# Token-major layer norms in the second half of a two-model float32 forward pass on one Trainium2 core

## The reference

```python
def layer_norm(x, g, b):
    xf = x.astype(jnp.float32)
    mu = jnp.mean(xf, axis=-1, keepdims=True)
    var = jnp.mean(jnp.square(xf - mu), axis=-1, keepdims=True)
    y = (xf - mu) * lax.rsqrt(var + LN_EPS) * g.astype(jnp.float32) + b.astype(jnp.float32)
    return y.astype(x.dtype)
...
    h = layer_norm(x, ln_in_g, ln_in_b)
    for l in range(DEPTH_2):
        mix = token_mix(h, positions, w_in[l], b_in[l], pool_w[l], pool_scale[l], w_pool_out[l],
...
        h = layer_norm(DEEPNORM_ALPHA * h + mix, ln1_g[l], ln1_b[l])
        ffn = conv_ffn(h, w_up[l], ffn_dw_w[l], ffn_dw_b[l], w_down[l])
        h = layer_norm(DEEPNORM_ALPHA * h + ffn, ln2_g[l], ln2_b[l])
    return h
```

## Time and profile before

| what | value |
|---|---|
| median of 3 runs (lowest, highest) | 2410.09 us (2407.65, 2414.35) |
| profiled execution: its own time | 2415.38 us |
| its span in the trace | 2413.2 us |
| PE busy | 2281.4 us, 95% |
| DVE, ACT, POOL busy | 1550.5, 1141.5, 348.5 us |
| mean granted PE clock | 0.962 of full speed |

### The profile page before, as it was taken

How to read it: one execution, slowest core, us unless ns; L and a number is a source line. 1 busy time by engine, 2 the same in 40 slices (tenths; PEclk the granted TensorE clock), 3 DMA queues, 4 the chain that set the end, 5 groups by cost and what they waited for, 6 DMA issues and landing times.

```text
span 2413.2 us, 45770 instructions
## 1 busy us (share of the span) xinstructions
PE 2281.4 (95%) x18326; PEld 2203.9 (91%) x18326; DVE 1550.5 (64%) x2039; ACT 1141.5 (47%) x1478; POOL 348.5 (14%) x448
## 2 busy tenths in 40 slices
PE   8999998999999999999999998988899998989998
PEld 7899997899999999999989997886899987878997
DVE  6865547665467775554876545866777466866764
ACT  5653345544355555433664434434365353445542
POOL 0011100022000000220301100930012038000110
PEclk9999998999999999999999999998999998889999
DMA  6356542366544444665435653542466542515651
GB/s 208 125 145 190 192 131 94 88 191 187 185 157 146 145 153 123 186 187 186 151 123 157 191 191 93 153 134 76 122 175 188 187 132 88 191 53 140 188 182 65
DMA packets 431038, 362.12 MB, mean 150 GB/s; under 512 B 20524, under 2 KB 404144, under 8 KB 430904
## 3 DMA queue, kind: packets, MB, share of 16 engines
q1 hardware_dynamic: 429128, 358.79, 48.5%
q0 software_dynamic: 1264, 0.71, 0.1%
q10 hardware_dynamic: 512, 0.72, 0.1%
HBM read 359.12 MB, written 1.05 MB: 149 GB/s over the span
## 4 chain that ended last, share of the span: by engine, by line
PE 79%; DVE 9%; POOL 6%; ACT 3%; issue 1%; DMA 0%; SPq 0%; ACTq 0%; POOLq 0%; DVEq 0%
PE bank L495 70%; POOL hT L1405 4%; DVE weights_lo L1984 3%; POOL Z L1407 2%; PE bank L598 2%; PE bank L526 1%; PE bank L842 1%; PE bank L1037 1%; PE bank L1069 1%; ACT weights_hi L1443 1%; PE bank L755 1%; PE bank L856 1%; PE bank L1050 1%; PE bank L779 1%; PE bank L733 0%
## 5 line engine op out<-in xcount | busy, mean ns | idle before, releaser
L1984 DVE TENSOR_TENSOR weights_lo<-weights,weights_hi 128x2048 fp32r<-128x2048 f32 x343 | 788.7, 2299 | 483.3 <-ACT weights_hi L1443 481.1
L495 PE MATMUL bank<-h_hi,weights_hi 128*128 128x256 f32 x3648 | 1045.3, 287 | 46.7 <-DVE h_lo L2524 16.6
L495 PE MATMUL bank<-h_lo,weights_hi 128*128 128x256 f32 x3648 | 1034.2, 283 | 0.0
L495 PE MATMUL bank<-h_hi,weights_lo 128*128 128x256 f32 x3648 | 1033.6, 283 | 0.0
L1443 ACT CAST weights_hi<-weights 128x2048 fp32r<-128x2048 f32 x343 | 654.5, 1908 | 524.6 <-PE bank L495 516.3
L495 PEld LDWEIGHTS bank<-h_hi,weights_hi 128*128 128x128 f32 x3648 | 701.6, 192 | 57.9 <-issue 51.4
L495 PEld LDWEIGHTS bank<-h_lo,weights_hi 128*128 128x128 f32 x3648 | 701.6, 192 | 1.5 <-issue 1.4
L495 PEld LDWEIGHTS bank<-h_hi,weights_lo 128*128 128x128 f32 x3648 | 701.0, 192 | 0.0
L495 PE MATMUL bank<-hid_hi,weights_hi 128*128 (+1 forms) x1056 | 295.5, 280 | 0.0
L495 PE MATMUL bank<-hid_lo,weights_hi 128*128 (+1 forms) x1056 | 295.4, 280 | 0.0
L495 PE MATMUL bank<-hid_hi,weights_lo 128*128 (+1 forms) x1056 | 295.4, 280 | 0.0
(11 more groups left out here) (350 smaller groups left out, 2738.9 us busy)
## 6 DMA issues: line engine op xcount, KB each, us to landing
weights<-in_f_w_gu SPq DMA_DIRECT2D x176, 512.0 KB, 5.0
weights<-in_f_w_out SPq DMA_DIRECT2D x88, 512.0 KB, 4.2
weights<-in_w_up SPq DMA_DIRECT2D x88, 512.0 KB, 4.9
weights<-in_w_in SPq DMA_DIRECT2D x82, 512.0 KB, 4.6
weights<-in_c_w_qkv SPq DMA_DIRECT2D x72, 512.0 KB, 4.5
weights<-in_a_w_qkv SPq DMA_DIRECT2D x48, 512.0 KB, 4.6
weights<-in_w_down SPq DMA_DIRECT2D x44, 512.0 KB, 4.1
weights<-in_a_w_o SPq DMA_DIRECT2D x16, 512.0 KB, 4.1
```

Of the source, the lines that this page charges most:

```text
L495: mm = nc.tensor.matmul(out, x, y, start=(first and n == 0), stop=(last and n == 2), skip_group_check=True)
L1984: v_.tensor_tensor(w_lo[slot][:], raw[slot][:], w_hi[slot][:].bitcast(F32), ALU.subtract).then_inc(lo_ready, 1)
```

## The change

The residual stream of the second model is kept with tokens in the partitions (`x_t`, the same memory as `xT`, read as 2 tiles of 128 tokens x 1024 features).

- The projections in front of a norm (`f_w_out` of the last layer, `w_o_2`, `w_down_2`) run through the new `deep_tokens`: the activations are the stationary operand, the weights the moving one, 512 columns per matmul, 24 matmuls per unit. The four banks are (token tile, half of the features).
- In the last feed-forward of the first model `residual_to_banks` puts the residual into the banks ahead of the projection, by 16 float32 matmuls with the identity.
- DVE's add (`add_tokens`) sums over features in its accumulator; ACT squares with the negative mean as bias and sums in its accumulator; mean, root and reciprocal are 128 x 1. The final RMS norm is folded in: squares straight from the banks, then one DVE instruction that scales and sums.
- The normalized rows are turned back by 16 transposes; DVE applies gain and offset as it takes them out of the banks, ACT rounds, DVE makes `h_lo`.
- POOL multiplies the gain into `x_t` and adds the offset (two instructions of 128 x 2048), `residual`, for the next norm's residual.
- SP loads the gains and offsets, repeated over the partitions, 512 KB each: 3 such loads in the first model's last feed-forward, 2 at the head and 2 at the tail of each `ffn2`.
- The last norm ends in token order, so `end` goes; four stores of 256 KB take the place of two of 512 KB.

```diff
+            def residual_to_banks():
+
+                for tt in range(NT):
+                    for half in range(2):
+                        x = open_item(2 * tt + half)
+                        for kk in range(4):
+                            nc.tensor.matmul(banks[x.bank][:, kk * P:(kk + 1) * P], xT[:, 4 * half + kk, tt * P:(tt + 1) * P],
+                                             ident[:], start=(kk == 0), stop=False, skip_group_check=True)
+                        token_items.append(x)
...
+            def deep_tokens(name, l, n_units, src, tag, bank0, ready, begun=()):
...
+                def step(u, n, last):
+                    w = parts(u, 1024)
+                    for tt in range(NT):
+                        for half in range(2):
...
+                            for j in range(2):
+                                mm = product(banks[x.bank][:], [y[:, (2 * n + j) * T + tt * P:(2 * n + j) * T + (tt + 1) * P] for y in src],
+                                             [y[:, j, 512 * half:512 * half + 512] for y in w], fresh and j == 0, last and j == 1)
+                            if last:
+                                close(mm, x, *([u] if tt + half == 2 else []))
...
-                if source:
-                    m = sums(at, xT, lambda j: pe.wait_ge(bank_free[source[j].bank], source[j].free))
-                else:
-                    m = sums(at, xT, lambda j: pe.wait_ge(y_ready, 2 * j + 2))
-                v = sums(at + 1, sq, lambda j: pe.wait_ge(squares_ready, count(squares_ready)))
...
+                            for kk in range(2):
+                                k = 2 * j + kk
+                                mm = nc.tensor.transpose(banks[at + j][:, kk * T + tt * P:kk * T + (tt + 1) * P],
+                                                         x_t[:, tt, k * P:(k + 1) * P], ident[:])
+                            if tt:
+                                close(mm, xs[j])
...
+                    if u.index in gains_at:
+                        where, g, b, l = gains_at[u.index]
+                        if l is None:
+                            sp.dma_start(final_gain, vector_row("final_norm", None)).then_inc(gains_landed[where], 16)
+                        for z, name in enumerate((g, b)):
+                            sp.dma_start(gains[where][:, z, :], vector_row(name, l)).then_inc(gains_landed[where], 16)
...
+            def residual(tag, where, landed_now):
+
+                x = items[tag][3]
+                pool.wait_ge(pe_done, x.done)
+                pool.wait_ge(gains_landed[where], landed_now)
+                g, b = (gains[where][:, z, :].unsqueeze(1).to_broadcast([P, NT, D]) for z in range(2))
+                gp.tensor_tensor(x_t[:], x_t[:], g, ALU.mult).then_inc(residual_scaled, 1)
+                n_residual[0] += 1
+                pool.wait_ge(residual_scaled, n_residual[0])
+                gp.tensor_tensor(x_t[:], x_t[:], b, ALU.add).then_inc(residual_ready, 1)
...
+                if tag[0] == "ln_in_g_2":
+                    for q, x in enumerate(source):
+                        done(x)
+                        fn(final_squared_at[q], banks[x.bank][:], ACT.Square, accum_out=final_squared[:, q:q + 1]).then_inc(final_squares, 1)
...
+                for tt in range(NT):
+                    act.wait_ge(centred, count(centred))
+                    fn(squared[tt], x_t[:, tt, :], ACT.Square, bias=nmean[:, tt:tt + 1],
+                       accum_out=std[:, tt:tt + 1]).then_inc(ln_squares, 1)
...
+            def add_tokens(q):
+
+                x, tt, half = source[0][q], q // 2, slice(512 * (q % 2), 512 * (q % 2) + 512)
+                total = sums_t[:, q:q + 1]
...
+                    ins = v_.scalar_tensor_tensor(x_t[:, tt, half], x_t[:, tt, half], source[1], banks[x.bank][:],
+                                                  ALU.mult, ALU.add, accum_out=total)
```

More of the change, by code:

```diff
@@ L1247, in mix @@
                 items["m", l] = it
[L1249 to L1264, removed]
             last_add = [None]
@@ L1331, in _ @@
             out = t["out"][0].rearrange("(t p) n -> p t n", p=P)
[L1332 to L1336, removed]
+            for q in range(2 * NT):
+                tt, half = q // 2, slice(512 * (q % 2), 512 * (q % 2) + 512)
+                sp.wait_ge(out_ready, q + 1)
+                sp.dma_start(out[:, tt, half], x_t[:, tt, half]).then_inc(out_stored, 16)
+            sp.wait_ge(out_stored, 16 * 2 * NT)
         @block.gpsimd
@@ L1824, in ln @@
                 if not last:
                     for k in range(KT):
-                        offset(h_hi, k).then_inc(hi_part, 1)
-                for k in range(KT):
-                    offset(xT, k).then_inc(y_ready, 1)
+                        if k % 2:
+                            freed(items[tag][k // 2])
+                        else:
+                            act.wait_ge(ln_ready, count(ln_ready))
+                        nc.scalar.copy(h_hi[:, k, :], hT[:, k, :]).then_inc(hi_part, 1)
@@ L2514, in ln @@
[L2514 to L2525 removed]
+                if tag[0] == "ln_in_g_2":
+                    dve.wait_ge(gains_landed["sq"], 48)
+                else:
+                    dve.wait_ge(residual_ready, count(residual_ready))
@@ new lines, in ln @@
+                if not last:
+                    at, ab = ROW[tag[0]] + tag[2], ROW[tag[1]] + tag[2]
+                    count(ln_ready, KT // 2)
+                    for k in range(KT + 2):
+                        if k < KT:
+                            x = items[tag][k // 2]
+                            if k % 2 == 0:
+                                done(x)
+                            ins = v_.tensor_scalar(hT[:, k, :], banks[x.bank][:, (k % 2) * T:(k % 2 + 1) * T],
+                                                   pcol[:, at + k:at + k + 1], pcol[:, ab + k:ab + k + 1], ALU.mult, ALU.add)
+                            if k % 2:
+                                free(ins, x)
+                            else:
+                                ins.then_inc(ln_ready, 1)
+                        if k >= 2:
+                            dve.wait_ge(hi_part, count(hi_part))
+                            v_.tensor_tensor(h_lo[:, k - 2, :], hT[:, k - 2, :], h_hi[:, k - 2, :].bitcast(F32),
+                                             ALU.subtract).then_inc(h_ready, 1)
@@ L2636, in mix @@
                                  ALU.add).then_inc(centred, 1)
+                count(centred)
                 rest_of(11)
@@ L2755, in _ @@
                     n_ffn += 1
-                elif kind == "end":
-                    if source[0]:
-                        for j in range(4):
-                            add_pair(j)
-                    for n, x in enumerate(items["end"]):
-                        done(x)
-                        free(v_.tensor_copy(xrows[:, n % 2, (n // 2) * 512:(n // 2 + 1) * 512], banks[x.bank][:]), x)
 def lambda_init(i):
```

205 lines of the change are left out of this document (126 added, 79 removed).

## The result

The changed kernel takes 2378.77 us (median of 4 runs, 2375.48 to 2382.74) beside 2409.11 for the kernel before (4 runs, 2407.65 to 2414.35): a ratio of 0.9867, with an interval of 0.9846 to 0.9889. It gained 30.3 us where I forecast 56. The direction was right; the time lies 5.8 us above the end of my range. The profiled execution took 2377.22 us with a span of 2375.4, which is 38 less than the profiled one of before. Of these 38, about 5 belong to that one execution of before: its own time of 2415.38 lies 5.3 above the median of 2410.09, and its last feed-forward took 191.82 where the one before it took 186.60.

The account below looks back on a forecast made before the run. PE, busy 95% of the span near full clock, was taken as the bound, with 84.1 us in five gaps. 18 + 16 + 12.6 + 15.2 - 3.8 - 2 = 56.0 off 2415.38 gave 2359.4, adjusted to 2354; range 2345 to 2373.

Parts of the forecast that it names:

- The wide matmuls, 15.2: Token-major projections: 512-column matmuls start 0.217 apart, saving 0.39 us per unit over 39 counted units, 15.2 us.
- 0 if the pace per column holds: Lower bound of the wide matmuls' saving: nothing gained if time goes by columns; upper bound 16 us.
- the rival that said so: Rival "Wide matmuls gain nothing": 512 columns bring no saving, time 2369 us; chance 14%.
- POOL's residual at nothing: POOL's two residual instructions, 9.2 us for both, hidden under some 20 us of cover before the gate product; cost 0.
- POOL is late: Rival: POOL, slowed beside DVE's splits and h_lo, overruns its cover by 4 to 6 us at two mixes, 2364; 8%.
- The inner norms, 18: Three norms inside the second model: PE's gap falls from 12.84 to 6.9 us, 6.0 saved each, 18 in all.
- Between the models, 16: RMS norm plus next norm between the models: PE's gap falls from 24.6 to 8.6 us, saving 16 (13 to 17).
- The end, 12.6: Tail after the last projection: 8.4 us against 21.0, saving 12.6 (10 to 13.5).
- The residual on PE, 3.8: First model's last feed-forward: 16 float32 matmuls, 32 passes, put the residual into the banks, costing 3.8 us.
- The clock, 2: After each norm PE starts at the low clock; 0.5 us added each for idling or transposing through the gap, 2 us.
- so that rival fell: Rival "The clock stays low longer": whole first unit at low clock, 2.5 us at four norms, 2364; chance 12%.
- The loads of the gains: Repeated gain rows, 3.7 to 5.6 us per group, hide in slack; rival that they load slowly: 2424 us, 4%.

Follow-up runs that it names:

- cut matmuls: Changed kernel with each 512-column matmul cut into two of 256 or, in a second kernel, four of 128: 2385.79 us and 2663.89 us (one run).
- `h_lo` taken from the bank: Changed kernel with the second model's h_lo computed from the PSUM bank times the gain, norm bias left out of it: 2363.16 us, ratio 0.9803 to the kernel before.
- putting the collision at two more norms: Changed kernel with the residual of both ln1 norms moved to right behind the norm's transposes: 2399.4 us, ratio 0.9951 to the kernel before.
- POOL later: Changed kernel with POOL's residual of ln_in and inner ln2 starting only after all eight h_lo are written: 2365.64 us, ratio 0.9817 to the kernel before.

## Why the prediction was wrong

It promised 56.0 us and 30.3 came: 25.7 short. By its own terms:

- **The wide matmuls, 15.2: wrong.** The step that failed is "the pace at 256 sits on a cost per matmul, its weight load". I took 0.217 for 512 columns from the float32 sums, an instruction of another kind, and the window with 136 columns as proof that fewer columns save nothing and so more would cost less. That inference needs 256 to lie on the floor. The cut matmuls show that it lies on the slope, just past the corner: the floor of 0.112 ends just below it, and beyond it the columns count in full. The bound "0 if the pace per column holds" was the true value, and the rival that said so had 14%.
- **POOL's residual at nothing: wrong in its mechanism.** I priced POOL's time and its cover before the gate product, and both were right: 4.5 and 4.6 us, ended at 1487.4, long before the gate product at 1506.7, which came 23.5 us into the mix and not 19.5, since PE had stood ahead of it. I read the 3.52 beside a split as DVE slowing POOL, and never turned it round to ask what POOL does to a DVE that stands on the path. The rival "POOL is late" put eight `h_lo` into POOL's time, where it should have put POOL's into theirs. The step that failed is "what I cost at nothing": the sum had no term for `h_lo` waiting on POOL's instruction. It measures 14.7 us in the two mixes by `h_lo` taken from the bank, and putting the collision at two more norms costs 19.
- **The inner norms, 18: right where nothing holds DVE.** Both `ln1` gaps are 6.85 beside 6.9 forecast. At `ln2` it is 10.3 and a second wait of 2.95; with POOL later 7.2.
- **Between the models, 16: right in the chain.** It is 13.1 in place of 8.6, and 9.05 with POOL later, so the chain was sized 0.4 too short.
- **The end, 12.6: right.** The last wide matmul is issued at 2366.94 and would have been followed at 2367.2; the span ends at 2375.4: 8.2 beside 8.4.
- **The residual on PE, 3.8:** right, 3.5 by its rows, and 4.5, roughly, by leaving it out.
- **The clock, 2: too dear.** In the first 21.9 us behind the four norms (`ln_in`, `ln1`, `ln2`, `ln1`) the kernel before issues 174, 174, 164 and 170 matmuls, and the one with POOL later 169, 184, 176 and 184. At three of the four it has more, and there its window's mean clock is 1.00. The changed kernel itself has 174 and 173 at the two `ln1`, as many as before or more. Idling or transposing through the whole gap didn't keep the clock low longer than sums did, so that rival fell. Where PE stood in the middle of the first unit, with POOL on the path, it was low for longer.
- **The loads of the gains:** they land in 6.2 to 8.9 us, and no ACT rounding waits for one. That rival fell too.

The two failed terms are 15.2 and 14.7, 29.9 together against the 25.7 that are missing. The 4 us left over go the other way: the clock's 2, which didn't come, and some 2 more. The traces say where to look for these: the changed kernel's first mix takes 219.6 us from its first matmul to the first of `w_o_2` (1483.16 to 1702.72) against 218.7 before (1491.61 to 1710.32), although its first 21.9 us hold 34 matmuls fewer, 4.0 us. So 3.1 us come back later in it, and I haven't traced how. That the sum of the misses comes out so near is partly luck.

## What to carry to other kernels

When work is moved to GpSimd, ask which VectorE instructions with both inputs in SBUF lie in the same microseconds: here one long GpSimd instruction stopped each of them until it ended. Cover for the GpSimd instruction itself says nothing about that. Let it start behind the critical ones, cut it in pieces, or give VectorE's instruction an input from PSUM; each of these won back 14 to 17 us here. Where a row shows one engine slowed by another, ask for the other direction too. And a pace read at one width is extrapolated only if it is known on which side of the corner between the cost of a matmul and the cost of a column that width lies: two matmuls of different width, on the side to which the change goes, tell it.

## What the runs showed of the hardware

- The hold between VectorE and GpSimd works in both directions and by whole instructions: `h_lo` 0.41 to 4.4, a split 2.29 to 6.5, GpSimd's 2048 columns 4.50 to 6.55, its 256 columns 0.73 to 2.79.
- Matmuls of the rounded halves (float32r in the kernel) at full clock take 0.456 ns a column at 256 and 512 columns, which is 1.09 clocks; read as two-byte values 0.443. At the low clock the 256-column ones start 0.213 apart (1483.51, 1483.72, 1483.93, 1484.15 in the changed kernel), one clock a column, and the 128-column ones start 0.213 apart too (four in 0.85): there the narrower matmul saves nothing at all.
- A stream of 128-column matmuls, each with its weight load, can stay at the low clock from its start to its end, as `w_o_2` did (granted clock 0.50), while the same stream in the feed-forward ran at full clock (1.00 from 1400 to 1420).
